# A two-network float32 kernel: lower parts of 65 weight blocks on GpSimd, new weights for its planner, turns of 128 columns, powers in halves

## The reference

```python
# first network, for l in 0, 1
x = x + 0.5 * swiglu(rms_norm(x, ffn1_norm[l]), ffn1_w_gate[l], ffn1_w_up[l], ffn1_w_down[l])   # 1024 -> 2816 -> 1024
h = rms_norm(x, mix_norm[l])
u = h @ w_in[l]
y_ssd, y_mla, y_conv = ssd_mixer(...), mla_mixer(...), conv_mixer(...)
x = x + concatenate([y_ssd, y_mla, y_conv]) @ w_out[l]
x = x + 0.5 * swiglu(rms_norm(x, ffn2_norm[l]), ffn2_w_gate[l], ffn2_w_up[l], ffn2_w_down[l])
# second network, for l in 0, 1: differential attention beside a chunked mLSTM, then
u = sigmoid(ga) * ya + sigmoid(gb) * yb
x = x + u @ w_o[l]
```

## Time and profile before

| | us |
|---|---|
| median of three runs | 1970.06 |
| lowest and highest run | 1969.53, 1972.91 |
| the profiled execution | 1969.57 |
| its span | 1967.7 |
| TensorE busy in the span | 1876.6 |
| VectorE busy | 1224.6 |
| ScalarE busy | 1053.3 |
| GpSimd busy | 106.0 |

### The profile page before, as it was taken

One profiled execution on the slowest core, in us unless ns is written; L12 is line 12 of the kernel. 1 busy time (PEld: TensorE's weight loads), 2 busy tenths in 40 slices (PEclk: granted clock), 3 DMA queues, 4 the chain that ended last, 5 costly groups with the idle time before them and its releaser, 6 DMA issues.

```text
span 1967.7 us, 24989 instructions
## 1 busy us (share of the span) xinstructions
PE 1876.6 (95%) x9884; PEld 1589.5 (81%) x9884; DVE 1224.6 (62%) x1786; ACT 1053.3 (54%) x1571; POOL 106.0 (5%) x83
## 2 busy tenths in 40 slices
PE   6999979899999999997999999999899999998999
PEld 5888879688888888897778888888688788877877
DVE  5555586765555555577765545597556569755754
ACT  5444656565444544465655444475565455656542
POOL 0000111000000000010200000020000000100000
PEclk9999989999999999998989999999999999999999
DMA  6555433235555555552324546553245545423553
GB/s 232 184 163 202 158 128 108 86 129 182 184 179 192 182 178 191 177 171 87 108 75 163 191 150 215 172 183 129 97 152 190 172 162 182 140 97 132 189 182 107
DMA packets 88532, 309.84 MB, mean 157 GB/s; under 512 B 9952, under 2 KB 10592, under 8 KB 88416
## 3 DMA queue, kind: packets, MB, share of 16 engines
q1 hardware_dynamic: 87552, 306.35, 46.1%
q10 hardware_dynamic: 720, 1.68, 0.2%
q0 software_dynamic: 144, 0.21, 0.0%
HBM read 307.16 MB, written 1.05 MB: 157 GB/s over the span
## 4 chain that ended last, share of the span: by engine, by line
PE 87%; DVE 8%; ACT 2%; issue 2%; DMA 1%; POOL 0%; DVEq 0%; SPq 0%; ACTq 0%
PE bank L1028 83%; PE bank L1025 4%; DVE WL L1833 2%; DVE XC L1977 1%; ACT WH L1402 1%; ACT PA L1402 0%; DMA X<-in_x_dram 0%; DVE STATS L2089 0%; DVE H L1925 0%; POOL CW L2526 0%; DVE STATS L2415 0%; DMA RAW<-in_WALL_dram 0%; DVE GA L1941 0%; DVE GA L1938 0%; ACT L1402 0%
## 5 line engine op out<-in xcount | busy, mean ns | idle before, releaser
L1833 DVE TENSOR_TENSOR WL<-RAW,WH 128x1024 fp32r<-128x1024 f32 (+2 forms) x602 | 707.5, 1184 | 508.9 <-ACT WH L1402 507.3
L1402 ACT ACTIVATE WH<-RAW 128x1024 fp32r<-128x1024 f32 (+2 forms) x602 | 614.0, 1030 | 602.6 <-PE bank L1028 595.8
L1028 PE MATMUL bank<-WH,XTH 128*128 128x512 f32 (+2 forms) x1440 | 557.9, 387 | 17.5 <-DVE WL L1833 17.5
L1028 PE MATMUL bank<-WH,XTL 128*128 128x512 f32 (+2 forms) x1440 | 550.7, 382 | 0.0
L1028 PE MATMUL bank<-WL,XTH 128*128 128x512 f32 (+2 forms) x1440 | 550.3, 382 | 0.0
L1028 PE MATMUL bank<-WH,FR 128*128 128x512 f32 x1136 | 353.3, 392 | 1.8 <-ACT QK L1402 1.8
L1028 PEld LDWEIGHTS bank<-WH,XTH 128*128 128x128 f32 x1440 | 274.5, 191 | 68.7 <-DVE WL L1833 18.8
L1028 PEld LDWEIGHTS bank<-WL,XTH 128*128 128x128 f32 x1440 | 273.5, 190 | 52.1
L1028 PEld LDWEIGHTS bank<-WH,XTL 128*128 128x128 f32 x1440 | 274.2, 190 | 50.5 <-issue 1.0
L1028 PEld LDWEIGHTS bank<-WH,FR 128*128 128x128 f32 x1136 | 211.2, 189 | 45.7 <-DVE WL L1833 2.2
L1028 PE MATMUL bank<-WL,FR 128*128 128x512 f32 x568 | 222.5, 392 | 0.0
(11 more groups left out here) (305 smaller groups left out, 1655.5 us busy)
## 6 DMA issues: line engine op xcount, KB each, us to landing
RAW<-in_WALL_dram SPq DMA_DIRECT2D x554, 512.0 KB, 3.2
RAW<-in_WALL_dram SPq DMA_DIRECT2D x38, 256.0 KB, 2.6
RAW<-in_WALL_dram SPq DMA_DIRECT2D x8, 448.0 KB, 3.4
X<-in_x_dram SPq DMA_DIRECT2D x2, 512.0 KB, 6.5
out_dram<-X SPq DMA_DIRECT2D x4, 256.0 KB, 2.1
CONSTS<-in_CST_dram ACTq DMA_DIRECT2D x1, 728.0 KB, 5.9
ROWP<-in_ROWP_dram ACTq DMA_DIRECT2D x1, 672.0 KB, 10.2
ROUNDED<-in_CSTR_dram POOLq DMA_DIRECT2D x1, 208.0 KB, 7.7
```

What stands on the lines that cost most here:

```text
L1028: return self.e.matmul(out, lhs, rhs, start=start, stop=stop, skip_group_check=True)
L1402: return self.e.activation(out, in_, func, **k)
L1833: self.e.tensor_tensor(lo, raw, hi.bitcast(F32), ALU.subtract).then_inc(*self.up("lo", j))
```

## The change

Seven edits.

- `WORK` gets other figures; blocks cost 272 ("tok") or 288 ("feat") units of TensorE and at least 60.
- A split counts as near when it is due within 400 units of its end and not 200; no split goes ahead of an eviction of a bank pair that could start at least as early.
- When VectorE's clock is more than 100 units past ScalarE's at the end of the rounding and GpSimd's is at most 50 past it, the planner gives the lower part of the block to GpSimd, at 200 units per 1024 numbers where VectorE has 99. That comes to 65 of 600 blocks. They have a semaphore of their own, for which TensorE waits.
- Three chains get a further dependency each: `decay` waits for `lat_y` before `cum`, a head waits for the product of the head two before it, and `finish` waits for Z's eviction. At the end the planner goes on until nothing is owed.
- The power of a tile's 16 sums becomes two, the half of K first; the factor of Q moves from `qk_norm` to `qk_gain`.
- The turns of Q and K take 128 columns from a flat view `QKX`, of which the first 96 are the head and the rest the next head's; the further 32 rows of the result are not read.

```diff
@@ WORK (of some 110 entries, those that differ most)
-    "rstd": "V30 G70", "cum": "P200 A60 V140", "ex": "P80 A30", "decay3": "V170 A50",
-    "qk_sum": "V195 G380", "qk_norm": "V115", "qk_rope": "V260", "sc": "P87 V100 A155",
-    "fin_var": "V15 G55", "cn_a": "P175 A100 V170", "as": "P95 V150 A235", "evict_ukv": "A160",
+    "rstd": "V34 G160", "cum": "P180 A60 V140", "ex": "P180 A30", "decay3": "V115 A45",
+    "qk_sum": "V195 G170", "qk_norm": "V96", "qk_rope": "V225", "sc": "P88 V90 A113",
+    "fin_var": "V16 G147", "cn_a": "P60 A215 V176", "as": "P147 V143 A202", "evict_ukv": "A126",
@@ Order.split
-        self.at["V"] = max(self.at["V"], self.at["A"]) + 20 + 99 * size // 1024
-        self.split_ends[j] = self.at["V"]
+        e = "V"
+        if self.at["V"] > self.at["A"] + 100 and self.at["G"] <= self.at["A"] + 50:
+            e = "G"
+            self.by_pool.add(j)
+        self.at[e] = max(self.at[e], self.at["A"]) + 20 + (99 if e == "V" else 200) * size // 1024
+        self.split_ends[j] = self.at[e]
@@ Order.turn
-            near = v + 120 + 200 >= self.at["P"] + 265 * (j - len(self.blocks))
-            if s <= min(when + 40 * near, limit):
+            near = v + 120 + 400 >= self.at["P"] + 265 * (j - len(self.blocks))
+            if s <= min(when + 40 * near, limit) and not (best and best.group[0][0] == "evict" and when <= s):
@@ Order.block
-        self.at["P"] = self.ends["block", j] = when + max(265 * size // 1024, 25)
+        self.at["P"] = self.ends["block", j] = when + max((272 if lin.kind == "tok" else 288) * size // 1024, 60)
@@ Order.mix: decay, head, finish
             yield "kpe", i
+            for t in range(2):
+                yield "lat_y", i, t
             yield [("cum", i)]
...
             yield [("sc", i, h)]
+            if h >= 2:
+                yield "pv", i, h - 2
             yield [("pt", i, h)]
...
             yield "mid", i, t
+            yield "evict", ("z", i, g)
             yield [("fin_y", i, t, g)]
@@ Kernel.allocate
+        self.QKX, _ = mk("QKX", [128, 3104], m)
         self.QK, m = mk("QK", [128, 2, 16, 96], m)
@@ PE.block
-        w.wait_ge(*self.at("lo", j))
+        w.wait_ge(*self.at("lo_pool" if j in k.order.by_pool else "lo", j))
@@ PE.qkt
-                m = self.tr(ps[0:96, 256 * x + 128 * t:256 * x + 128 * t + 128], k.QK[:, t, g + x, :])
+                at = 1536 * t + 96 * (g + x)
+                m = self.tr(ps[:, 256 * x + 128 * t:256 * x + 128 * t + 128], k.QKX[:, at:at + 128])
@@ Vector.split, Vector.qk_norm, Vector.qk_gain
+        if j in k.order.by_pool:
+            return
...
-        w.wait_ge(*self.at("rsqrt_pool", ("qk", i, t)))
-        e.tensor_scalar(k.stat(("scq", i), 16)[:, 8 * t:8 * t + 8], st[:, 0:8], 96 ** -0.5, None, ALU.mult)
+        w.wait_ge(*self.at("rsqrt_pool", ("k", i, t)))
...
+        w.wait_ge(*self.at("rsqrt_pool", ("q", i, t)))
+        e.tensor_scalar(k.stat(("scq", i), 16)[:, 8 * t:8 * t + 8], k.stat(("qk", i, t), 16)[:, 0:8], 96 ** -0.5, None, ALU.mult)
@@ Pool.qk_sum, Pool.split
-        self.rsqrt(("qk", i, t), 16)
+        w.wait_ge(*self.at("var_dve", ("qk", i, t)))
+        for name, n in (("k", 8), ("q", 0)):
+            self.e.tensor_tensor(st[:, n:n + 8], st[:, n:n + 8], k.HM[:, 0:8], ALU.pow).then_inc(*self.up("rsqrt_pool", (name, i, t)))
...
+    def split(self, j):
+        k, w = self.k, self.w
+        if j in k.order.by_pool:
+            raw, hi, lo = k.split_of(j)
+            w.wait_ge(*self.at("hi", j))
+            self.e.tensor_tensor(lo, raw, hi.bitcast(F32), ALU.subtract).then_inc(*self.up("lo_pool", j))
```

More of the change, by code:

```diff
@@ L227, in __init__ @@
         self.pairs, self.held, self.freed = [(0, 1), (2, 3), (4, 5)], [], {}
-        self.stages, self.chains = stages, []
+        self.stages, self.chains, self.by_pool = stages, [], set()
         self.at = {e: 0 for e in "PAVG"}
@@ L244, in __init__ @@
                 self.hyb(i, st[1])
-        while self.chains:
-            assert self.turn(NEVER)
+        while self.turn(NEVER):
+            pass
+        assert not self.chains
         self.add("end")
@@ L2485, in program @@
             "fin_var": self.fin_var, "hyb_load": self.hyb_load,
-            "hq_sum": self.hq_sum, "hb_sum": self.hb_sum, "oan_var": self.oan_var,
+            "hq_sum": self.hq_sum, "hb_sum": self.hb_sum, "oan_var": self.oan_var, "split": self.split,
         }
@@ L2540, in qk_sum @@
     def qk_sum(self, i, t):
-        self.rsqrt(("qk", i, t), 16)
+        k, w = self.k, self.w
+        st = k.stat(("qk", i, t), 16)
+        w.wait_ge(*self.at("var_dve", ("qk", i, t)))
+        for name, n in (("k", 8), ("q", 0)):
+            self.e.tensor_tensor(st[:, n:n + 8], st[:, n:n + 8], k.HM[:, 0:8], ALU.pow).then_inc(*self.up("rsqrt_pool", (name, i, t)))
     def mo_var(self, i, t):
```

## The result

The changed kernel takes 2016.68 us (median of 4 runs, 2016.21 to 2018.76) against 1969.8 (4 runs): a ratio of 1.0237, 95% interval 1.022 to 1.0255. It is 47 us slower, where 1954 was forecast and the range ended at 1983. The sign was rival A's, its size was more than twice A's.

The account below looks back on a forecast made before the run. TensorE was taken as the bound, busy 1876.6 of 1967.7 us, leaving idle time and low-clock losses to win. Terms +5 - 10 - 7.5 - 2 - 2 = -16.5 from 1969.57 gave 1953.1, stated as 1954, range 1925 to 1983.

Parts of the forecast that it names:

- rival A: Before the mixers' attention and in hybrid layers, the shared SBUF interface decides, 0.4 us per lower part: slower, 1987; chance 0.2.
- Lower parts on GpSimd: Subtractions moved off VectorE, 13 on the path before the mixers' attention at 0.4 us net loss: +5 us (-16 to +26).
- The order: New weights, earlier splits, evictions first and dependencies only move idle time: -10, -7.5, -2 and -2 us across mixers and hybrid layers.
- the wait for QK: Before each mixer's attention, blocks fill TensorE's idle time: 5 of 12.0 us back in each, -10 (0 to -24).
- the exponential waits: TensorE's other waits for the attention's exponentials, 9.8 us in all: a fifth won by a block ahead, -2 us.
- the waits for lower parts: TensorE's waits for weight blocks; in each hybrid layer half of 7.5 us won, -7.5 in all (0 to -15).
- Turns of 128 columns and half powers: Wider Q and K transposes and powers split in halves, in the mixers: each costed at 0.
- B: Idle time only moves: Q and K waits are VectorE's total work, softmax latencies reappear one block on; 1970, chance 0.13.
- C: The order does nearly all it can before the attention and in hybrid layers, GpSimd 0: 1921, chance 0.15.

Follow-up runs that it names:

- the first experiment: The changed kernel with the same written list of phases, but VectorE instead of GpSimd makes the 65 lower parts: 1960.36 us, ratio 0.9947 to the kernel before.
- the version without GpSimd: The changed kernel with the GpSimd choice taken out of the planner, so the list too is planned for VectorE alone: 1940.9 us, ratio 0.9852 to the kernel before.

## Why the prediction was wrong

**The step that failed** is the term "Lower parts on GpSimd", +5 us, and in it two sizes and a count; the mechanism stood there and was right. It turned the sign of the whole sum.

- "a net loss of about 0.4 us": measured on one and the same list, VectorE is held up 1.94 us for each subtraction and saved 1.21, a net loss of 0.74. The duration was mis-sized: I took 1.98 us from the skip product, one of whose inputs is 16 constants, each repeated, and not from the product at 360.83, whose 3.27 us contain a wait for VectorE until 361.89: 3.27 - 1.06 = 2.2, nearer to the 2.5 measured. And the held-up time per product (1.6) grows with the duration: 2.5 less the half microsecond that VectorE needs itself.
- "if half of them move, 13 in all, the path gets 13 x 0.4": 65 cost 0.87 us each in the mean. The rule picks a block when VectorE is behind, and there the delay goes through to TensorE. My 13 were all in the mixers; 35 of the 65 lie in the hybrid layers, whose TensorE I took for full and VectorE for able to catch up. On one list they cost 40.6 us there and 18.4 in the mixers. What VectorE had to spare there was no cover for holdups of 2 us.
- The low clock behind longer idle stretches was left out of that term: TensorE busy 14.6 us more.

So the term is +56.3 where I had +5, with +26 as its upper bound. VectorE's net loss is 48 us of it (1266.6 - 1218.8); which part of the rest is the low clock and which is idle time of another kind isn't separated. (In the prediction's chances, 0.11 and 0.02 for "same" are 0.13 and not 0.12.)

**The order.** I had -21.5. The list that the changed kernel runs gives -10.2 (the first experiment); a list planned for the engines that then do the work gives -29.6. The difference, 19.5 us, may be a second cost of GpSimd's lower parts, before any instruction runs: the planner believed that 65 lower parts cost VectorE nothing. That isn't shown, since near at 600 alone moved the time by 16 us without any of them. By places: the wait for QK fell from 9.5 to 6.4 us a mixer in the version without GpSimd (I took 5 of 12 back, with the low clock), the exponential waits from 9.8 in all to 4.5 (I took a fifth), the waits for lower parts from 20.7 to 9.3, 6.1 of them at the very start (I took half of the hybrid layers' 11.4; it was nearly all). Together: -10.2 + 56.3 = 46.1 of the 46.9 measured.

**What held.** Turns of 128 columns and half powers: nothing, as costed. In the changed kernel the four halves take 7.83 us, 1.96 each, and queue in front of six lower parts. VectorE's instructions lengthened beside GpSimd's, as the forecast said they would, and the 63 subtractions of 128x1024 took 2.37 to 3.20 us. The stretch before the attention went past 36 us, which was the mark of rival A; of the two waits of 5.7 us for a lower part in the hybrid layers one stayed in the changed kernel, and both are gone in the version without GpSimd.

**The rivals.** A had the mechanism and the sign, with the same 0.4 that was too small: 1987. The statement against it, that five slots of WH lie between, was no defence, since a held-up VectorE is late with all that stands in its own queue, and in the stretch shown that is the taps and the rotation. The rule of the Trainium skill that the prediction cites (SBUF — State Buffer, "Who interferes with whom") is that a VectorE instruction with two SBUF inputs and a GpSimd instruction that reads SBUF take one shared interface, and that the second is blocked until the first is done. The runs agree for the subtractions. For the powers they don't: a power of 12 columns reads SBUF too and lasts 2.51 us, and no conv tap took over 489 ns in the run with 65 of them. The measurement decides: how long a GpSimd instruction lasts doesn't tell how long it holds VectorE up. B and C, on the order alone, lie on either side of what the runs without GpSimd gave.

**What stays open.** The order's gain isn't a sum of its parts. Lists with all edits but one gave 1974.1, 1976.1 and 1963.0, the kernel before with none of them 1970, and near at 600 gave 1956.9. None of the three was added alone to the kernel before, so what one is worth by itself isn't known; 1940.9 is the one list of several that fell well. Whether measured weights or the longer lead are right in general can't be said from them. The three dependencies and half powers weren't taken out of it one by one. Nor do the runs say why a block costs TensorE twice as much in a hybrid layer as in a mixer, though VectorE is held up about as long for it in both (1.8 to 2.0 us).

## What to carry to other kernels

Work moved to GpSimd to relieve a full VectorE can make VectorE slower: look first at whether both stream two tensors from SBUF, and count what VectorE is held up for (here 1.94 us a piece) against what it is spared (1.21). A rule that picks such work by VectorE's backlog picks the places where it costs; where it was free, in the feed-forward stages, it wasn't needed. And an edit that is a gain can hide in a change that is a loss: the same change without GpSimd's lower parts is 1.5% faster than the kernel before.

## What the runs showed of the hardware

A GpSimd subtraction of 128x1024 float32 numbers took 2.53 us in the mean, and back to back they let through one VectorE instruction of two SBUF inputs each, whether it needs 0.34 or 0.5 us. A GpSimd power of 12 columns, whose two inputs lie in SBUF too, took as long, 2.51 us, and cost VectorE nothing. VectorE was held up 1.94 us for each subtraction on one list and 1.97 on another; the kernel's time went up in proportion to their number, by some 0.87 us each. In the feed-forward stages the same subtraction took 2.42 us and cost 7 us of VectorE in all for 65.
